# State-space mixer with the sample states laid out by feature, and the norm's squares taken inside the MLP's up-projection

## The reference, cut to what matters

```
h = h + mixer(rms_norm(h, w1))
h = h + relu(rms_norm(h, w2) @ w_up)**2 @ w_down      # rms_norm: x * rsqrt(mean(x*x) + eps) * w
# SSD, for one token of a sample: state s[head] is 64 features x 128
s = exp(dt * A) * s + (dt * x)[:, None] * B[None, :]
y = s @ C + d_skip * x
```

## Time and profile before

| what | value |
|---|---|
| median of 3 runs | 1866.49 us (1859.41 to 1867.5) |
| the profiled execution, its own time | 1868.64 us |
| its span in the trace | 1866.8 us |
| granted TensorE clock, mean | 0.967 |
| TensorE busy | 1774.9 us, 95% of the span |
| weight loads | 1482.3 us, 79% |
| VectorE busy | 1022.2 us, 55% |
| ScalarE busy | 389.1 us, 21% |
| GpSimd busy | 129.1 us, 7% |

### The profile page before, as it was taken

One profiled execution on the slowest core, in us unless ns is written; L12 is line 12 of the kernel. 1 busy time (PEld: TensorE's weight loads), 2 busy tenths in 40 slices (PEclk: granted clock), 3 DMA queues, 4 the chain that ended last, 5 costly groups with the idle time before them and its releaser, 6 DMA issues.

```text
span 1866.8 us, 22734 instructions
## 1 busy us (share of the span) xinstructions
PE 1774.9 (95%) x8378; PEld 1482.3 (79%) x8378; DVE 1022.2 (55%) x1893; ACT 389.1 (21%) x964; POOL 129.1 (7%) x205
## 2 busy tenths in 40 slices
PE   6999999898999999999999999999999999999994
PEld 5776747776888888878788888888878888888884
DVE  4443764456454354545557777778552653454553
ACT  2332101112310022001223432333310230012100
POOL 1000310000000000000110111101100000000001
PEclk9999998898999999998979999999999999999997
DMA  7111531024536746441333334332322332443211
GB/s 268 66 57 47 187 122 47 13 77 152 217 154 225 289 184 247 180 159 36 136 127 128 102 127 149 141 126 101 147 94 77 147 136 113 158 158 136 102 57 46
DMA packets 50247, 244.23 MB, mean 131 GB/s; under 512 B 7624, under 2 KB 10776, under 8 KB 45040
## 3 DMA queue, kind: packets, MB, share of 16 engines
q1 hardware_dynamic: 37392, 123.75, 19.2%
q0 software_dynamic: 12624, 119.21, 16.4%
q10 hardware_dynamic: 144, 0.09, 0.0%
HBM read 227.56 MB, written 82.53 MB: 166 GB/s over the span
## 4 chain that ended last, share of the span: by engine, by line
PE 86%; DVE 8%; issue 2%; ACT 2%; DMA 1%; DVEq 0%; POOL 0%; ACTq 0%; SPq 0%
PE bank L935 41%; PE bank L541 29%; PE bank L1102 2%; DVE ss L2010 1%; PE bank L1024 1%; DVE conv L1928 1%; PE bank L643 1%; PE bank L627 1%; PE bank L1008 1%; DVE rstd L1463 1%; PE bank L686 1%; PE bank L1029 1%; DMA ring<-units 1%; DVE yrstd L1966 1%; PE bank L777 1%
## 5 line engine op out<-in xcount | busy, mean ns | idle before, releaser
L541 PE MATMUL bank<-hn,ring 128*128 128x260 f32 x2304 | 558.9, 396 | 14.0 <-DVE ss L2010 6.6
L541 PEld LDWEIGHTS bank<-hn,ring 128*128 128x128 f32 x2304 | 436.5, 195 | 89.1 <-issue 17.5
L935 PE MATMUL bank<-hid,ring 128*128 128x260 f32 x1024 | 231.0, 382 | 0.0
L935 PEld LDWEIGHTS bank<-hid,ring 128*128 128x128 f32 x1024 | 194.6, 190 | 29.9
L935 PE MATMUL bank<-hid,ssum 128*128 128x260 f32 x768 | 174.2, 382 | 0.0
L935 PEld LDWEIGHTS bank<-hid,ssum 128*128 128x128 f32 x768 | 145.9, 190 | 22.4
L935 PE MATMUL bank<-hn,ring 128*128 128x260 f32 x512 | 125.0, 387 | 5.6 <-DVE hnt L1745 5.6
L935 PE MATMUL bank<-hnt,ring 128*128 128x260 f32 x512 | 124.0, 385 | 0.0
L935 PE MATMUL bank<-hnt,ssum 128*128 128x260 f32 x512 | 120.1, 387 | 2.5 <-DVE hid L1774 2.5
L1765 DVE TENSOR_TENSOR u<-bank,p1c 128x260 f32<-128x260 f32 x48 | 20.6, 429 | 184.2 <-PE bank L935 182.5
L935 PEld LDWEIGHTS bank<-hn,ring 128*128 128x128 f32 x512 | 98.2, 192 | 21.7 <-DVE hnt L1745 6.4
(11 more groups left out here) (350 smaller groups left out, 2148.3 us busy)
## 6 DMA issues: line engine op xcount, KB each, us to landing
ring<-units SPq DMA_DIRECT2D x224, 512.0 KB, 4.2
seg<-cums POOLq DMA_DIRECT2D x8, 1024.0 KB, 4.7
ss<-ssm POOLq DMA_DIRECT2D x8, 1024.0 KB, 7.5
xb<-sxs POOLq DMA_DIRECT2D x8, 1024.0 KB, 5.0
out_ssm<-ss POOLq DMA_DIRECT2D x8, 1024.0 KB, 5.9
out_win_k<-cache_k POOLq DMA_DIRECT2D x8, 1022.0 KB, 8.7
out_win_v<-cache_v POOLq DMA_DIRECT2D x8, 1022.0 KB, 6.6
gath<-cache_k POOLq DMA_DIRECT2D x12, 256.0 KB, 5.1
```

What stands on the lines that cost most here:

```text
L541: x = mm(half(n), ring[:, s, k], src[:, first + k, cols], start=start and k == blocks[0], stop=last and k == blocks[-1])
L935: x = mm(bank[:, 0:LO], weight(m, w, q % (DC // 2)), operand(m, q), start=q == 0 and m not in (2, 3), stop=q == every - 1, skip_group_chec ...
```

## The change

**The sample states** get features on the partitions: `ss0` is [128 features, 2 halves of the group, 8 samples, 128 state entries]. Decays and steps (dt) of each feature and sample are columns of the table `tabg`. ScalarE multiplies the states by the decays, 16 activations of 128x128, at the beginning of its part of the group, before the exponentials of the scan. `ssamp`, now B and C of the samples in place of x, is what goes through HBM and comes back as `xb`. VectorE makes the step in 16 instructions of 128x128 and then y itself, as 16 multiply-and-sum instructions of 128x128 (`sample_y`), behind the four masks of seg. TensorE's 16 matmuls and GpSimd's two multiplications are gone. The order of ScalarE's convolution work within a group changes as well.

**The squares of the MLP's norm**: ScalarE now writes h times the weight (`weigh_turns`) while the output projection runs. The squares are taken into a buffer of their own (`hsq`) during the first four up-quads, two blocks after each, and VectorE adds them there. TensorE's `norm(r, SUMS)` moves behind quad 3, and std is made behind VectorE's part of quad 4.

```
-TAB = F_SAMPLE + CJ * NB
+F_STEP = F_SAMPLE + 2 * NB
+TAB = F_STEP + 2 * NB
...
 # POOL, per group
                 if g:
                     pool.wait_ge(sem("ssm_out"), g * 16)
+                    pool.wait_ge(sem("ssm_read"), g)
                 pool.dma_start(flat(ss0[:]), A["ssm0"][g]).then_inc(sem("ssm_in"), 16)
-                pool.wait_ge(sem("sxdt_ready"), g + 1)
-                pool.dma_start(sxs[g].rearrange("(b c) -> b c", b=NB), flat(sxdt[:])).then_inc(sem("rows_out"), 16)
+                pool.wait_ge(sem("ssamp_read"), g + 1)
+                pool.dma_start(sxs[g].rearrange("(b c) -> b c", b=NB), flat(ssamp[:])).then_inc(sem("rows_out"), 16)
...
-                for half in (slice(0, NB // 2), slice(NB // 2, NB)):
-                    ...
-                    nc.gpsimd.tensor_tensor(s, s, decays.to_broadcast((P, NB // 2 * CJ, CHD)), ALU.mult).then_inc(
-                        sem("ssm_decayed"), 1)
-                pool.wait_ge(sem("ssm_read"), g + 1)
+                pool.wait_ge(sem("ssm_stepped"), g + 1)
                 pool.dma_start(A["ssm1"][g], flat(ss0[:])).then_inc(sem("ssm_out"), 16)
...
 # PE
-                        if c == 0 and f == 0:
+                        if c == 0 and f == SQUARES_IN - 1:      # SQUARES_IN = 4
                             norm(r, SUMS)
...
-                project(3, sample_y(g, d, products))
+                project(3)
...
 # ACT
+            def weigh_turns(r, t_written):
                 for k in range(DC):
                     act.wait_ge(copied[(t_written + k) % 2], turns_before(t_written + k) + 1)
-                    squared(k)
+                    run(hn[:, k], h[:, k], ACT.Copy, scale=norms[:, r, k]).then_inc(hn_ready, 1)
+            def squared_late(r, k):
+                if k >= 2:
+                    act.wait_ge(squares_added, r * DC + k - 1)
+                run(hsq[:, k % 2], h[:, k], ACT.Square).then_inc(squares, 1)
...
                             relu_squared(hid[:, f, 5], hid[:, f, 5])
+                            if c == 0 and f < SQUARES_IN:
+                                squared_late(2 * layer + 1, 2 * f)
+                                squared_late(2 * layer + 1, 2 * f + 1)
...
 # ACT, mix(g, d, nxt), behind btok
-                if nxt is not None:
-                    conv_in(nxt, 0)
-                    conv_tanh(nxt, 1 - d, 0)
-                    conv_in(nxt, 1)
-                    conv_tanh(nxt, 1 - d, 1)
                 act.wait_ge(sem("ssamp_read"), g + 1)
+                act.wait_ge(sem("ssm_in"), g * 16 + 16)
+                for i in range(2):
+                    for b in range(NB):
+                        own = F_SAMPLE + NB * i + b
+                        last = i and b == NB - 1
+                        run(ss0[:, i, b], ss0[:, i, b], ACT.Copy, scale=tabg[:, own:own + 1]).then_inc(
+                            sem("ssm_decayed") if last else mstep, 1)
                 act.wait_ge(sem("cums_in"), g * 16 + 16)
                 # the four exponentials efeat, unchanged
                 # before: bounded(2); then per head: bounded(next), exp, and behind the second
                 # head conv_in(2), conv_tanh(2); at the end conv_in(3), conv_tanh(3)
+                # after: bounded(2), conv_in(0), bounded(3), exp, conv_tanh(0), exp, bounded(0),
+                # conv_in(1), bounded(1), exp, conv_tanh(1), exp, conv_in(2), conv_tanh(2), ...
...
 # DVE
                         up(c, f)
-                        if c == 0 and f == 0:
+                        if c == 0 and f < SQUARES_IN:
+                            add_square(r, 2 * f, True)
+                            add_square(r, 2 * f + 1, True)
+                        if c == 0 and f == SQUARES_IN:
                             # norm_summed, then std as before
...
             for j in range(DC):
                 residual(T_OUT0B + j, j, U_OUT0 + j + 1)
-                add_and_weigh(1, j)
-                if j % 2:
-                    dve.wait_ge(hn_ready, HN_BEFORE[1] + j + 1)
-                    pair_hn(j // 2)
-                if j in (4, 6):
-                    sum_weights(BASE0, j // 2 - 2)
+                if j in (3, 5):
+                    sum_weights(BASE0, j // 2 - 1)
+                if j % 2 == 0 and j:
+                    dve.wait_ge(hn_ready, HN_BEFORE[1] + j)
+                    pair_hn(j // 2 - 1)
...
+                mdo(V.tensor_tensor(sxd[:], conv[:, d, 0:2, TP:T],
+                                    tabg[:, F_STEP:F_STEP + 2 * NB].rearrange("p (i b) -> p i b", i=2), ALU.mult))
...
+                def step_states():
+                    dve.wait_ge(sem("sx_in"), g * 16 + 16)
+                    dve.wait_ge(sem("ssm_decayed"), g + 1)
+                    for i in range(2):
+                        for b in range(NB):
+                            mdo(V.scalar_tensor_tensor(ss0[:, i, b], xb[:, b, 0], sxd[:, i, b:b + 1], ss0[:, i, b],
+                                                       ALU.mult, ALU.add),
+                                "ssm_stepped" if i and b == NB - 1 else None)
+                def sample_y():
+                    for i in range(2):
+                        for b in range(NB):
+                            mdo(V.tensor_tensor_reduce(yprod[:], ss0[:, i, b], xb[:, b, 1], 1.0, 0.0, ALU.mult,
+                                                       ALU.add, ysamp[:, i, b:b + 1]),
+                                "ssm_read" if i and b == NB - 1 else None)
+                    mdo(V.tensor_tensor(yT[:, :, TP:T], yT[:, :, TP:T], ysamp[:], ALU.add))
...
                 for i, j in enumerate((2, 3, 0, 1)):
                     dve.wait_ge(sem("seg_expd"), g * 4 + (i + 1))
                     mdo(V.tensor_tensor(seg[:, j], seg[:, j], cbm[:], ALU.mult), "seg_ready")
-                dve.wait_ge(sem("ssm_read"), g + 1)
-                mdo(V.tensor_tensor(yT[:, :, TP:T], yT[:, :, TP:T],
-                                    B[6][:, 0:2 * NB].rearrange("p (i b) -> p i b", i=2), ALU.add), "sample_y_read")
+                sample_y()
```

More of the change, by code:

```diff
@@ L90 @@
 FQ = FC // CHUNKS // 2
+SQUARES_IN = 4
 DQ = DC // 2
@@ L262, in build @@
         hid = sb("hid", [P, FQ, 7, LO], stack=m)
+        hsq = sb("hsq", [P, 2, T], stack=m)
         m.close()
@@ L295, in build @@
         ssamp = sb("ssamp", [NB, 2, P], stack=c)
-        sxdt = sb("sxdt", [NB, CJ, CHD], stack=c)
-        ss0 = sb("ss0", [P, NB, CJ, CHD], stack=c)
+        sxd = sb("sxd", [P, 2, NB], stack=c)
+        ysamp = sb("ysamp", [P, 2, NB], stack=c)
+        yprod = sb("yprod", [P, P], stack=c)
+        ss0 = sb("ss0", [P, 2, NB, P], stack=c)
         yout = sb("yout", [P, 2 * CG, T], stack=c)
@@ L997, in ssd_cb @@
                 x.then_inc(sem("cb_ready"), 1)
[L999 to L1012, removed]
             def ssd_intra(g):
@@ L1046, in ssd_norm, with ssd_mix @@
                 x.then_inc(sem("ysq_summed"), 1)
-            def ssd_mix(g, d, project, products=2 * DC):
+            def ssd_mix(g, d, project):
                 if not isinstance(g, int) or g > 0:
@@ L1396, in mix, with decays @@
                 heads = (2, 3, 0, 1)
+                def decays(i):
+                    act.wait_ge(sem("seg_bounded"), g * 4 + (i + 1))
+                    run(flat(seg[:, heads[i]]), flat(seg[:, heads[i]]), ACT.Exp, scale=-1.0).then_inc(
+                        sem("seg_expd"), 1)
                 bounded(heads[0])
-                for i, j in enumerate(heads):
-                    if i + 1 < CJ:
-                        bounded(heads[i + 1])
-                    act.wait_ge(sem("seg_bounded"), g * 4 + (i + 1))
-                    run(flat(seg[:, j]), flat(seg[:, j]), ACT.Exp, scale=-1.0).then_inc(sem("seg_expd"), 1)
-                    if i == 1 and nxt is not None:
-                        conv_in(nxt, 2)
-                        conv_tanh(nxt, 1 - d, 2)
-                if nxt is not None:
+                if nxt is not None:
+                    conv_in(nxt, 0)
+                bounded(heads[1])
+                decays(0)
+                if nxt is not None:
+                    conv_tanh(nxt, 1 - d, 0)
+                decays(1)
+                bounded(heads[2])
+                if nxt is not None:
+                    conv_in(nxt, 1)
+                bounded(heads[3])
+                decays(2)
+                if nxt is not None:
+                    conv_tanh(nxt, 1 - d, 1)
+                decays(3)
+                if nxt is not None:
+                    conv_in(nxt, 2)
+                    conv_tanh(nxt, 1 - d, 2)
                     conv_in(nxt, 3)
@@ L1438, in _ @@
             run(by_group(F_DEC, NT), by_chunk(NT * CH_ALL, NT), ACT.Exp).then_inc(sem("tab_begun"), 1)
-            run(by_group(F_SAMPLE, NB), by_chunk(2 * NT * CH_ALL, NB), ACT.Exp).then_inc(sem("tab_begun"), 1)
+            for e in range(2):
+                rows = slice(CHD * e, CHD * e + CHD)
+                of_half = B[5][:].rearrange("p (k b g i e) -> p k e g i b", k=2, b=NB, g=CG, i=2)[rows]
```

(20 more changed lines are left out.)

61 lines of the change are left out of this document (26 added, 35 removed).

## The result

The changed kernel took 1872.58 us (median of 9 executions, 1866.97 to 1879.96), the kernel before 1858.41 in the same rounds (9 executions, 1853.68 to 1867.5): a ratio of 1.0063, 95% interval 1.0043 to 1.0084. It is slower, by 0.6% (the two medians by themselves are 14.2 us or 0.76% apart). The forecast of 1877 was an absolute time, made on a profiled execution of 1868.64, which turned out 10 us above the longer series' median; against the median known then, 1866.49, it was +0.56%.

A forecast was written before the change was run, and what follows sets the result against it. It took TensorE to bound the kernel before, VectorE's list the middle groups after. Middle groups +18, last -3.6, group 0 -2.5, layer 0 -5, layer 1 +3.1 gave +10: 1879 us profiled, 1877 as median, range 1849 to 1894.

The forecast's parts named there:

- VectorE's list becomes the bound: Middle mixer groups: states kept 47.1 us after S, the start of the group's turns; TensorE idles 4.0, period 0.8 longer.
- Rival 2: Mixer: TensorE stays the bound, states ready at S + 43, period 54 or below, total 1832 us; chance 0.08.
- Rival 3: Mixer: the small VectorE and ScalarE instructions cost more than taken, total 1892 us; chance 0.12.
- y's place: VectorE's list in a group: y stands ahead of the states, so its 5.4 us delay what TensorE next waits for.
- The clock, 2.2 a group: Inter and project(5): after 4.0 us idle TensorE's clock drops, costing 2.2 us per group, between 1.3 and 3.0.
- rival 1: Mixer: VectorE binds but TensorE's clock holds, so no clock loss, total 1860 us; chance 0.25.
- Rival 5: Mixer: the clock stays low through intra too, each group losing twice as much, total 1895 to 1905; chance 0.05.
- The six middle groups: Mixer: 0.8 us of longer period plus 2.2 of clock loss in each of six groups, +18 us.
- The last group, -3.6: Last mixer group: no convolution beside it, so it gains what leaves TensorE, -3.6 us.
- Group 0, -2.5: First mixer group with the new tables: ScalarE's 16 activations first wait for the state load; -2.5 us taken.
- The squares: MLPs: layer 0's entry gains 11 us, each wait behind quad 3 costs 6; layer 0 -5, layer 1 +3.1.
- rival 4: Layer 0's entry gain is missed as weights arrive no earlier, -11 becomes -3, total 1885 us; chance 0.07.

The follow-up runs named there:

- e1: Mixer's part of the change alone, the squares left as in the kernel before: 1874.06 us, ratio 1.0064 to the kernel before.
- e4: Changed kernel with VectorE's loop over the six middle groups written out, same instructions and order: 1866.47 us, ratio 1.003 to the kernel before.
- e11: Changed kernel with 14 of the 16 multiply-and-sums of y taken out per group: 1845.15 us, ratio 0.9902 to the kernel before.
- e3: Changed kernel with y's multiply-and-sums moved behind the chunk states in VectorE's list: 1865.33 us, ratio 1.0023 to the kernel before.
- e7: e4 with 8 useless matmuls ahead of the inter step in all groups but the last: 1859.64 us, ratio 0.9992 to the kernel before.
- e14: The kernel before, unchanged, run again for a second trace: median 1860.67 us, the profiled execution 1864.18.
- e5: Changed kernel with TensorE's norm(r, SUMS) behind quad 4 and std behind VectorE's part of quad 5: 1858.73 us, ratio 0.9984 to the kernel before.
- e13: Kernel before with group 0's 16 state matmuls ahead of project(3) instead of between its matmuls: 1862.55 us, ratio 0.9991.

## Why the prediction was right

The direction and the mechanism were right: work taken from TensorE came back as idle time, because VectorE's list became the bound, and the idle time cost clock. The total agrees better than its terms do, which is in part luck.

*VectorE's list becomes the bound* (forecast): right. The copies were forecast at S + 11.1 and S + 17.1; the taps behind them start at S + 10.9 and S + 17.0. The steps took 6.16 us (6.1 forecast) and y 5.34 (5.4, at 0.34 each). The states are kept at S + 46.8 (S + 47.1). TensorE is idle for 3.55 us before the inter step (4.0). VectorE is busy 48.7 to 50.3 (51). A group without loss of clock was forecast at 58.3; it takes 58.1 with the loop (e1) and 57.8 without (e4). Rival 2 falls, as the states were not ready at S + 43; e11, with a list 4.7 us shorter, shows that its condition would have given 54.25, close to the 54 that it named. Rival 3 falls with 0.30, 0.385 and 0.334 for the three small forms. The 0.30 (16 in 4.80, from start to start) is below the 0.41 that the prediction worked out from the Trainium skill's budget for one activation (ScalarE: Activation LUTs, Rules for kernel authors); no run here shows one such activation by itself.

*y's place.* The prediction said that it fails if y's place in the list costs TensorE nothing. By e3 the place decides at which wait TensorE loses the time, and by e11 the length of the list decides that it loses it. The forecast of the period used both, and only the length is needed.

*The clock, 2.2 a group:* the mechanism was right (rival 1 falls, e7), the size somewhat large. Against the 58.07 of a clean group the four middle groups without a turn lose 2.09, 1.43, 1.74 and 1.51, a mean of 1.7. In e4 a group loses 0 to 2.7. Rival 5, which has twice the loss in every group, falls with this.

*The loop's turn* stood at nothing in the prediction, whose rows show no such wait. The six middle groups come to +17.4 (361.91 from group 1's start to group 7's, against 344.47), where +18 was forecast. They divide into 3.9 of list (six times 58.07 - 57.41), 6.8 of loss in the four groups without a turn, and 6.7 in the two with one. Of all this, 9.4 us is TensorE's own work taking longer (322.4 us busy against six times the 52.17 of a clean group). So the list's term and the clock's were each too large, and the turns, which weren't foreseen, filled the gap.

*The last group, -3.6:* 57.7 to 54.18, -3.5; TensorE has no wait in it.

*Group 0, -2.5:* 69.71 to 62.67, -7.0. The term was set against the one trace of before, whose group 0 ran project(3) at 0.50; against e14's 58.82 it is +3.9. The prediction knew that ScalarE's 16 activations wait for the load there, but not that the copies behind them would then hold VectorE and TensorE: 6.13 us of wait on ScalarE became 5.26 on TensorE, and intra behind it took 4.06 (2.57 in e14). The row with the clock at 0.50 was there to be read as well, and the prediction didn't look at group 0 by itself.

*The squares:* the first quad is over at 438.3, within the 434 to 439 named. From the first matmul of the second half of the output projection (L876, at 401.00; before L879, at 398.35) to there it is 37.3 us, before 49.5: -12.2 (12.4 worked out, 11 taken), so rival 4 falls. The wait behind quad 3 is 3.61 and 3.62 (3.8). Behind it, from 478.91 to 489.77 is 10.86 us where the same records at full clock take 7.9, so 3.0 of clock (2.2 forecast; the 6 taken becomes 6.6). Layer 0 with everything ahead of group 0 went from 904.09 to 899.24, -4.85, where -5 was forecast, but so close an agreement is luck: 2.65 us were lost ahead of that first matmul, in stages that the change doesn't touch (398.35 against 401.00), and from there on it is -7.5. Traces of the kernel before differ by more than that at the same point (404.24 in e14). Layer 1 with the rest: +4.3 (+3.1).

The sum of the traces is -4.85 - 7.0 + 17.4 - 3.5 + 4.3 = +6.3, the difference of the spans. The medians differ by 14.2. Against e14's trace (span 1862.4) the same sum is -9.6 (group 0 starts at 908.85) + 3.9 + 17.5 - 1.0 (all behind group 7's start) = +10.7, and both executions of the old kernel lie above their medians, by 10.2 and 3.5. So the gap between 6 and 14 comes largely from which execution was profiled, and group 0 is the largest single piece of it; which stages differ in the many executions without a trace stays open.

## What to carry to other kernels

Work that leaves the engine that is the bound is only gained as far as the engine that takes it has room in its own ordered list *between two hand-overs back*, not in the mean: VectorE had 13.7 us free per group and no room for 7.3. Add up the list from hand-over to hand-over, then price the idle time that results twice, once as time and once as lost clock. If such a wait can't be removed, useless matmuls in it can be worth more than nothing (7 us here). And a reduction's last matmul belongs a stage behind its last input: moving it and what VectorE makes of it by one quad took 14 us off this kernel.

## What the hardware showed that was not expected

At a turn of VectorE's loop the changed kernel and its variants e1, e5 and e11 show 3.80 to 4.03 us of idle time that is put to no engine. The kernel before has no such row, nor has any kernel with the loop written out. It is tempting to call the longer body the cause (75 instructions of VectorE in the group's window in the earlier trace rows, 112 and 117 after, 85 in a clean group of e11), and the instruction queue q14 moved 41 packets in the changed kernel, 28 before and 32 in e4. But e3 speaks against length alone: it has the same instructions in another order, the same loop and 42 such packets, and at its turns VectorE is idle for 2.97 and 2.77 us, put to TensorE, like the 2.27 to 2.89 at its other groups. Whether the turn's time was hidden in that wait isn't shown. Writing the loop out removes the idle time (e4); what it consists of stays open.

The same idle time does not always cost the same: 3.32 and 3.33 us before the same 12 matmuls gave 1.60 and 2.93, and 1.90 and 1.72 before project(3) of group 0 gave 19.8 and 10.8. In the slower of the last two the clock stood at 0.50 through nearly all of project(3) with its interleaved matmuls of one column, though TensorE was busy all the time (10.00 of 10 us in the window shown), and rose only behind it. In e13, without the interleaving, 32 records took 8.90 behind the row of small ones, a loss of 1.7. (The Trainium skill, TensorE: Matmul & The Clock Gate, Part 1, says that the ramp differs from run to run of one kernel; these traces agree, but here the spread is 9 us and more in a single stage.)
